# An encoder layer whose routing step is spread over the output projection, with another choice of the four experts and another first gather

## The chip, the core and the metric

One NeuronCore of a Trainium2 chip runs the whole layer in one launch. The metric is the time of that launch on the device in microseconds (us). The kernel before was timed three times: 1300.25, 1304.65 and 1307.12 us, so its median is 1304.65 us. TensorE is called PE here, VectorE DVE, ScalarE ACT, GpSimd POOL, and SP is the engine whose queue issues the weight loads.

## The reference

For 256 tokens x of 1024 features, the reference computes in fp32:

```
x = x + token_mixer(rmsnorm(x, g_mix), ...)      # SSD branch and attention branch, gated, then @ w_out
h = rmsnorm(x, g_ffn)
logits = h @ w_router + b_router                 # 256 x 32
top_val, top_idx = top_k(logits, 4)
top_w = softmax(top_val)
y[token] = sum over its 4 experts e of top_w * (act(h @ w_mlp1[e] + b_mlp1[e]) @ w_mlp2[e] + b_mlp2[e])
act(gate, up) = min(gate, 7) * sigmoid(1.702 * min(gate, 7)) * (clip(up, -7, 7) + 1)
out = rmsnorm(x + y, g_final)
```

The weights of the 32 experts are 32 x (1024x2048 + 1024x1024) fp32 numbers, 403 MB in all. Each is read once.

## The kernel before

**Two stages share one ring of weights.** `ring` holds 16 slots of 1 MB. The mixer works in 36 units (lines 433 and 436), each one slot of weights with 32 TensorE instructions; units 32 to 35 (`U_O` and up) are the output projection, and after each of them DVE adds half of the product to the residual rows `xres` (line 1162). The MoE stage works in 384 units, 12 for each expert: 8 "up" units (a slice of 128 rows of `w_mlp1`) and 4 "down" units (256 rows of `w_mlp2`). All of them are loaded by SP with `dma_start` at line 328. The first 16 loads wait for slots that the mixer gives up, the last of them for the end of unit 35. Load u+16 waits in `unit_used` (line 265) until TensorE has done its products with unit u. The loads stand in one queue in the order of the units.

**An expert on TensorE (lines 666 to 687).** It multiplies the 8 up units (line 629), transposes the result (line 663) once ACT has copied it out of PSUM (lines 906 and 908), adds the weighted result of the expert before to the sums in PSUM (`combine`, line 624), gathers the tokens of the next expert (line 611), and multiplies the 4 down units. The gather is a product of a 0/1 matrix `slotP` with three bf16 pieces (`hb1`, `hb2`, `hb3`) of the normed rows, 48 instructions.

**The routing step between the stages.** Everything in it waits for unit 35, in this order:

1. ACT squares the residual rows (line 883), POOL makes the reciprocal root (lines 953 and 954), DVE scales the rows into `hN` (line 1166).
2. PE transposes `hN` (line 416), DVE scales it with `g_ffn` into `hT` (line 995), PE multiplies the router (line 591).
3. DVE adds the bias, takes the eight largest of each row (line 1178), marks those above the fourth and those equal to it, and breaks ties with a scan (lines 1183 to 1196), which gives the mask `msk`.
4. PE counts the tokens of each expert with fp32 products (lines 596 to 600) and transposes the weights `wtok` (line 603). DVE subtracts for `hb3` (line 1206), turns the counts into ranks (lines 1209 to 1214) and places the tokens of expert 0 (lines 1227 to 1229).
5. ACT makes the three bf16 pieces in turn with DVE (lines 886, 888, 895, 1171, 1206).
6. PE gathers expert 0 (line 611), and then multiplies the weights with `b_mlp2` (line 698) into the four sums in PSUM. Only then begins the first up unit.

TensorE takes its instructions in order, so each item holds all that stand behind it. In the output projection it waits for all four parts of `hT` (`mix_ready`, 4) ahead of unit 32. DVE writes these parts in turn at lines 1153, 1154 and 1156. The last of ACT's transfers is `g_final` into `gfin` (line 899), issued after the third bf16 piece and the copy of the weights.

## Time and profile before

| what | us |
| --- | --- |
| median of the three timed runs | 1304.65 |
| span of the profiled execution | 1303.6 |
| the profiled execution's own time | not listed; the span is 1.05 below the median |
| PE busy | 1182.3 |
| DVE busy | 364.2 |
| ACT busy | 193.1 |
| POOL busy | 19.9 |

The span runs from the first to the last instruction. An engine's busy share is a mean over both stages. TensorE's instructions overlap each other, so a busy time of a line is not the time that the line takes; the difference of two start times is. An fp32 product is two instructions in the trace.

### The profile page before, as it was taken

What the parts mean: (1) busy time and instruction counts of PE and PEld (TensorE: products, weight loads), DVE (VectorE), ACT (ScalarE), POOL (GpSimd) and SP (SyncE); (2) the same over time, 40 slices, a digit from 0 to 9 for tenths busy, and PEclk for the clock granted to TensorE, in tenths of its full rate; (3) what the DMA queues carried; (4) which work ended last, traced back from release to release, by engine and by line L of the source; (5) the groups of instructions that cost most, each with busy time, mean ns of one, the idle gap of its engine ahead of it and who ended that gap; (6) DMA issues with size and microseconds to landing.
All of it is one profiled execution on the core that took longest, in us unless ns stands there. A gap on an engine that the chain in (4) does not pass through costs nothing.

```text
span 1303.6 us, 18034 instructions
## 1 busy us (share of the span) xinstructions
PE 1182.3 (91%) x6734; PEld 578.6 (44%) x6734; DVE 364.2 (28%) x1018; ACT 193.1 (15%) x362; POOL 19.9 (2%) x32
## 2 busy tenths in 40 slices
PE   5999999998799999989998988888899989998885
PEld 5888888887433333333333333333333333333331
DVE  2515788121412221222121111111122212111112
ACT  1212344001111110111011100100111011001001
POOL 0001111000000000000000000000000000000000
PEclk9999999999699999999999999999999999999998
DMA  9944322654099999999999999999999999999994
GB/s 283 281 142 117 128 97 97 230 217 171 29 417 417 417 417 417 417 417 418 417 418 418 418 418 418 418 418 417 417 417 418 418 418 418 418 418 417 418 417 178
DMA packets 113351, 445.18 MB, mean 342 GB/s; under 512 B 9731, under 2 KB 46947, under 8 KB 80515
## 3 DMA queue, kind: packets, MB, share of 16 engines
q1 hardware_dynamic: 109408, 441.48, 85.0%
q10 hardware_dynamic: 3907, 3.21, 0.9%
q8 instruction: 24, 0.39, 0.1%
q14 instruction: 12, 0.10, 0.0%
HBM read 443.61 MB, written 1.05 MB: 341 GB/s over the span
## 4 chain that ended last, share of the span: by engine, by line
PE 40%; DMA 37%; SPq 16%; issue 2%; DVE 2%; ACT 1%; ACTq 1%; DVEq 0%; POOL 0%; POOLq 0%
DMA ring<-in_w_mlp_dram 37%; SPq L328 16%; PE bank L433 14%; PE bank L629 14%; PE bank L436 5%; PE bank L624 1%; PE bank L611 1%; PE bank L562 1%; PE bank L552 1%; PE bank L698 1%; PE bank L524 1%; PE bank L416 1%; PE bank L663 0%; PE bank L591 0%; PE bank L515 0%
## 5 line engine op out<-in xcount | busy, mean ns | idle before, releaser
L629 PE MATMUL bank<-ring,arena 128*64 128x512 f32 x3072 | 702.7, 600 | 63.7 <-DMA ring<-in_w_mlp_dram 63.6
L629 PEld LDWEIGHTS bank<-ring,arena 128*64 128x64 f32 x3072 | 203.0, 137 | 515.3 <-issue 324.2
L1245 DVE TENSOR_TENSOR arena<-bank,b1T 128x256 f32<-128x256 f32 x128 | 53.8, 420 | 624.3 <-PE bank L663 621.9
L433 PE MATMUL bank<-hT,ring 128*128 128x256 f32 x576 | 128.3, 384 | 0.8 <-DVE hT L995 0.8
L433 PEld LDWEIGHTS bank<-hT,ring 128*128 128x128 f32 x576 | 110.9, 193 | 16.6 <-DVE hT L995 1.2
L436 PE MATMUL bank<-ring,hT 128*128 128x256 f32 x320 | 72.1, 386 | 2.2 <-DVE hT L1156 2.2
L906 ACT ACTIVATE arena<-bank 128x512 f32<-128x512 f32 x32 | 19.1, 597 | 362.4 <-PE bank L629 362.3
L436 PEld LDWEIGHTS bank<-ring,hT 128*128 128x128 f32 x320 | 61.5, 194 | 11.1 <-DVE hT L1156 2.6
L624 PE MATMUL bank<-arena 64*128 64x512 f32 x264 | 65.6, 615 | 0.8 <-ACT arena L916 0.8
L611 PEld LDWEIGHTS bank<-slotP,hb 128*128 128x128 bf16 x1536 | 47.7, 99 | 27.1 <-issue 23.5
L611 PE MATMUL bank<-slotP,hb 128*128 128x64 bf16 x1536 | 51.5, 195 | 3.1 <-DVE arena L1229 3.1
L663 PE MATMUL bank<-cst,arena 128*128 128x128 f32 x256 | 40.6, 286 | 14.4 <-ACT arena L906 9.6
L663 PEld LDWEIGHTS bank<-cst,arena 128*128 128x128 f32 x256 | 26.8, 140 | 47.1 <-ACT arena L906 36.1
L1227 DVE TENSOR_SCALAR slotP<-cst,rankm 128x64 bf16<-128x64 f32 x64 | 15.8, 247 | 96.9 <-ACT arena L914 96.9
L911 ACT ACTIVATE arena<-arena 128x256 f32<-128x256 f32 x64 | 26.7, 417 | 80.5 <-DVE arena L1248 80.4
L916 ACT ACTIVATE arena<-bank 128x512 f32<-128x512 f32 x32 | 19.1, 598 | 105.5 <-PE bank L629 105.5
L914 ACT ACTIVATE arena<-bank 128x256 f32<-128x256 f32 x32 | 12.3, 384 | 140.8 <-PE bank L618 140.8
L624 PEld LDWEIGHTS bank<-arena 64*128 64x128 f32 x264 | 22.7, 186 | 22.6 <-issue 20.9
L906 ACT ACT_TABLE_LOAD x8 | 10.3, 1283 | 134.4 <-PE bank L629 134.4
L433 PE MATMUL bank<-arena,ring 128*128 128x256 f32 x128 | 28.3, 380 | 0.5 <-ACT arena L867 0.5
L1251 DVE SCALAR_TENSOR_TENSOR arena<-arena 128x256 f32<-128x256 f32 x64 | 27.2, 426 | 2.4 <-DVE arena L1249 0.2
L433 PE MATMUL bank<-over,ring 128*128 128x256 f32 x128 | 27.8, 379 | 0.0
(204 smaller groups left out, 634.3 us busy)
## 6 DMA issues: line engine op xcount, KB each, us to landing
ring<-in_w_mlp_dram SPq DMA_DIRECT2D x384, 1024.0 KB, 22.1
ring<-in_w_in_dram SPq DMA_DIRECT2D x24, 1024.0 KB, 10.3
ring<-in_w_br_attn_dram SPq DMA_DIRECT2D x4, 1024.0 KB, 4.9
ring<-in_w_br_ssm_dram SPq DMA_DIRECT2D x4, 1024.0 KB, 5.0
ring<-in_w_out_dram SPq DMA_DIRECT2D x4, 1024.0 KB, 5.0
xres<-in_x_dram ACTq DMA_DIRECT2D x1, 1024.0 KB, 4.9
out_dram<-hN SPq DMA_DIRECT2D x2, 512.0 KB, 2.7
cst<-shape_constants_dram ACTq DMA_DIRECT2D x1, 736.0 KB, 6.4
```

Source lines behind the costliest of these rows:

```text
L328: sp.dma_start(dst, src).then_inc(slot_full[s], 16)
L433: last = nc.tensor.matmul(o, w[:, k, a * P:(a + 1) * P], rhs[:, k, :], start=(k == 0), stop=(k == KD - 1))
L436: last = nc.tensor.matmul(o, tokens[:, k, a * P:(a + 1) * P], w[:, k, :], start=(k == 0), stop=(k == KD - 1))
L611: last = nc.tensor.matmul(bank[b][:, k * CAP:(k + 1) * CAP], hb[part][:, t, k * P:(k + 1) * P], slotP[:, par, t, :], start=(t == 0 and par ...
L624: return nc.tensor.matmul(bank[b0 + q][:, :], slotWT[rows, (q // 2) * P:(q // 2 + 1) * P], ysb[rows, :], start=start, stop=stop, skip_grou ...
L629: return nc.tensor.matmul(bank[b][side * CAP:(side + 1) * CAP, :], tokens, w, start=start, stop=stop, skip_group_check=True)
L663: last = nc.tensor.transpose(bank[b][:, j * P:(j + 1) * P], hs[:, b * 512 + j * P:b * 512 + (j + 1) * P], ident)
L906: nc.scalar.activation(hs[:, 0:512], bank[0][:, :], ACT.Copy).then_inc(hs_ready, 1)
L911: nc.scalar.activation(sg[:, h * 256:(h + 1) * 256], ga[:, h * 256:(h + 1) * 256], ACT.Sigmoid, scale=ALPHA).then_inc(sg_ready, 1)
L916: nc.scalar.activation(ysb, bank[2][:, :], ACT.Copy).then_inc(ys_ready, 1)
L1245: step(V.tensor_tensor(o.rearrange("p (m s) -> p m s", m=4), bank[b][:, half].rearrange("p (m s) -> p m s", m=4), bias[:, m0:m0 + 4].unsqu ...
L1251: step(V.scalar_tensor_tensor(u_, u_, 1.0, g_, ALU.add, ALU.mult))
```

## The change

- Unit 32 takes its eight slices of `hT` as they come, two at a time (`first_out_unit`).
- The residual rows are transposed raw, in four quarters, and each quarter is multiplied with the router. The quarters stand in TensorE's order behind the units of the output projection, up to two units later. ACT squares each quarter as it comes, DVE copies and scales seven of the eight slices, ACT the last one.
- The norm's factor is applied to the logits, in the instruction that adds the bias, and not to the rows.
- The mask comes from two `match_replace` instructions and a comparison instead of comparisons, a sum, a scan and a product.
- The counts are bf16 products. Ranks are counted from 1, so the memset and the subtraction go.
- Expert 0 is gathered in one fp32 product from `xres` with a matrix `slot0` that carries the norm's factor, in two halves; the three bf16 pieces are wanted only from expert 1 on.
- The products with `b_mlp2` stand inside expert 0, in the place of its `combine` (which had added zeros), and TensorE waits there for the third bf16 piece. The transfer of `gfin` waits for that piece too.
- The first four experts are written out ahead of TensorE's loop.

```diff
...
+        lgt = lg36[:, :, 0:NE]
+        left36 = arena[:, 6984:7056].rearrange("p (t e) -> p t e", t=TT)
...
+        slot0 = slotW[:, 1, :, 0:CAP]
...
+        msk = sb("msk", [P, TT, NE], BF16, at=place_of["arena"] + 4 * 9488)
...
-            pe.wait_ge(mix_ready, 4)
-            for n in range(U_O, N_MIX):
-                unit(n, tokens=hT)
...
+            def first_out_unit():
...
+                for u in range(4):
+                    pe.wait_ge(mix_ready, u + 1)
+                    for a in range(2):
+                        for k in (2 * u, 2 * u + 1):
+                            last = nc.tensor.matmul(bank[n % 2][:, a * 256:(a + 1) * 256], hT[:, k, a * P:(a + 1) * P], w[:, k, :],
+                                                    start=(k == 0 and a == 0), stop=(k == KD - 1), skip_group_check=True)
+                last.then_inc(unit_done, 1)
+
+            def x1_transposes(u):
+
+                pe.wait_ge(unit_taken, U_O + u + 1)
+                for kk in range(2):
+                    o = bank[0][:, 0:256] if (u, kk) == (3, 1) else bank[2 + u][:, kk * 256:(kk + 1) * 256]
+                    for t in range(TT):
+                        last = nc.tensor.transpose(o[:, t * P:(t + 1) * P],
+                                                   xres[:, t, u * UW + kk * P:u * UW + (kk + 1) * P], ident)
+                last.then_inc(h2T_psum, 1)
...
+            def router(u):
+
+                pe.wait_ge(h2T_ready, u + 1)
+                for k in (2 * u, 2 * u + 1):
+                    if k == KD - 1:
+                        pe.wait_ge(x1T_last, 1)
+                    for t in range(TT):
+                        last = nc.tensor.matmul(bank[6][:, t * NE:(t + 1) * NE], x1T[:, k, t * P:(t + 1) * P], wr[:, k, :],
+                                                start=(k == 0 and t == 0), stop=(k == KD - 1), skip_group_check=True)
+                return last
+
+            first_out_unit()
+            unit(U_O + 1, tokens=hT)
+            x1_transposes(0)
+            unit(U_O + 2, tokens=hT)
+            x1_transposes(1)
             pe.wait_ge(late_in, 16 * 2)
-            for t in range(TT):
+            router(0)
+            unit(U_O + 3, tokens=hT)
+            x1_transposes(2)
+            router(1)
+            x1_transposes(3)
+            router(2)
+            router(3).then_inc(lg_psum, 1)
+
+            pe.wait_ge(msk_ready, 1)
+            nc.tensor.matmul(bank[7][:, 0:NE], m_leb[:, :], msk[:, 0, :], start=True, stop=True)
+            nc.tensor.matmul(bank[7][:, NE:2 * NE], onesb[:, :], msk[:, 0, :], start=True, stop=False)
+            nc.tensor.matmul(bank[7][:, NE:2 * NE], m_leb[:, :], msk[:, 1, :], start=False, stop=True).then_inc(rank_psum, 1)
+            nc.tensor.matmul(bank[4][:, 0:NE], onesb[:, :], msk[:, 0, :], start=True, stop=False)
+            nc.tensor.matmul(bank[4][:, 0:NE], onesb[:, :], msk[:, 1, :], start=False, stop=True).then_inc(cnt_psum, 1)
+
+            def first_gather():
+
+                pe.wait_ge(p_ready, 1)
                 for k in range(KD):
-                    last = nc.tensor.matmul(bank[6][:, t * NE:(t + 1) * NE], hT[:, k, t * P:(t + 1) * P], wr[:, k, :],
-                                            start=(k == 0), stop=(k == KD - 1))
-            last.then_inc(lg_psum, 1)
-
-            pe.wait_ge(w_ready, 1)
-            nc.tensor.matmul(bank[7][:, 0:NE], m_le, msk[:, 0, :], start=True, stop=True)
-            nc.tensor.matmul(bank[7][:, NE:2 * NE], ones, msk[:, 0, :], start=True, stop=False)
-            nc.tensor.matmul(bank[7][:, NE:2 * NE], m_le, msk[:, 1, :], start=False, stop=True)
-            nc.tensor.matmul(bank[7][:, 2 * NE:3 * NE], ones, msk[:, 0, :], start=True, stop=False)
-            nc.tensor.matmul(bank[7][:, 2 * NE:3 * NE], ones, msk[:, 1, :], start=False, stop=True)
...
-            for t in range(TT):
-                last = nc.tensor.transpose(bank[0][0:NE, t * P:(t + 1) * P], wtok[:, t, 0:NE], ident)
-            last.then_inc(wT_psum, 1)
+                    for t in range(TT):
+                        last = nc.tensor.matmul(bank[3 - k // 4][:, (k % 4) * CAP:(k % 4 + 1) * CAP], xres[:, t, k * P:(k + 1) * P],
+                                                slot0[:, t, :], start=(t == 0), stop=(t == TT - 1))
+                    if k == 3:
+                        last.then_inc(x0_psum, 1)
+                last.then_inc(x_psum, 1)
 
             def gather(par, b):
...
+
+                pe.wait_ge(wT_ready, 1)
+                pe.wait_ge(route_ready, 1)
+                for t in range(TT):
+                    for hf in range(2):
+                        nc.tensor.matmul(bank[SUMS + 2 * t + hf][:, :], wT[:, t * P:(t + 1) * P],
+                                         b2s[:, hf * 512:(hf + 1) * 512], start=True, stop=False, skip_group_check=True)
+
...
+                if first:
+                    pe.wait_ge(x0_half, 1)
+                else:
+                    pe.wait_ge(x32_ready, e + 1)
                 for q in range(KD):
+                    if first and q == 4:
+                        pe.wait_ge(x32_ready, e + 1)
                     up_unit(i, c, q)
                 for b in range(2):
                     pe.wait_ge(hs_ready, 2 * e + (b + 1))
                     transposes(b).then_inc(t_psum, 1)
-                pe.wait_ge(ys_ready, e + 1)
-                for q in range(4):
-                    combine(q)
...
+            for c in range(BODY):
+                expert(0, c, first=(c == 0))
...
+                act.wait_ge(unit_taken, U_O + u + 1)
+                for t in range(TT):
+                    nc.scalar.activation(hs[:, (2 * u + t) * UW:(2 * u + t + 1) * UW], xres[:, t, u * UW:(u + 1) * UW], ACT.Square,
+                                         accum_out=ssq[:, t, u:u + 1]).then_inc(x1sq_ready, 1)
+            act.wait_ge(h2T_psum, 4)
+            nc.scalar.activation(x1T[:, KD - 1, :], bank[0][:, 0:256], ACT.Copy,
+                                 scale=prmT[:, R_GFFN + KD - 1:R_GFFN + KD]).then_inc(x1T_last, 1)
+
+            act.wait_ge(x1r_ready, 1)
             for t in range(TT):
-                nc.scalar.activation(hN[:, t, :], xres[:, t, :], ACT.Square, accum_out=stat[:, 20 + t:21 + t]).then_inc(x1sq_ready, 1)
-
-            act.wait_ge(h2_ready, 2)
...
+            act.wait_ge(lmax_ready, 1)
+            for t in range(TT):
+                last = nc.scalar.activation(expl[:, t, :], lgt[:, t, :], ACT.Exp, bias=stat[:, 26 + t:27 + t])
+            last.then_inc(lexp_ready, 1)
+            act.wait_ge(wT_psum, 1)
+            nc.scalar.activation(wT[:, :], bank[6][0:NE, 0:SEQ], ACT.Copy).then_inc(wT_ready, 1)
             act.wait_ge(res_ready, 1)
             nc.scalar.activation(hb2[:, :, :], hs, ACT.Copy).then_inc(hb_ready, 1)
...
             nc.gpsimd.tensor_tensor(stat[:, 34:36], stat[:, 34:36], stat[:, 40:42], ALU.pow).then_inc(yr_ready, 1)
-            pool.wait_ge(x1sq_ready, 2)
+            pool.wait_ge(x1sum_ready, 1)
...
+            def x1T_copy(u):
+                dve.wait_ge(h2T_psum, u + 1)
+                kk = 2 if u < 3 else 1
+                V.tensor_tensor(x1T[:, 2 * u:2 * u + kk, :], bank[2 + u][:, 0:kk * 256].rearrange("p (k l) -> p k l", k=kk),
+                                prmT[:, R_GFFN + 2 * u:R_GFFN + 2 * u + kk].unsqueeze(2).to_broadcast([P, kk, SEQ]),
+                                ALU.mult).then_inc(h2T_ready, 1)
+
+            V.memset(slotWT, 0.0).then_inc(pw_ready, 1)
+            V.memset(lg36[:, :, NE:NE + 4], NO_LOGIT)
+            V.tensor_copy(m_leb[:, :], m_le)
+            V.tensor_copy(onesb[:, :], ones)
...
+                if u >= 1:
+                    x1T_copy(u - 1)
+            dve.wait_ge(x1sq_ready, 2 * 4)
+            V.tensor_reduce(stat[:, 20:22], ssq[:, :, :], AXX, ALU.add).then_inc(x1sum_ready, 1)
+            x1T_copy(3)
...
+            dve.wait_ge(lg_psum, 1)
+            dve.wait_ge(vec_in, 16 * 7)
             for t in range(TT):
...
+                last = V.scalar_tensor_tensor(lgt[:, t, :], bank[6][:, t * NE:(t + 1) * NE], r_tok[t], brt_b, ALU.mult, ALU.add)
+            link(last)
             for t in range(TT):
                 last = V.max(top8[:, t, :], lgt[:, t, :])
...
+            V.tensor_scalar(stat[:, 26:28], top8[:, :, 0:1].rearrange("p t a -> p (t a)"), -1.0, None, ALU.mult).then_inc(lmax_ready, 1)
+            link(V.memset(top8[:, :, TOPK:8], NO_LOGIT))
...
+                last = V.match_replace(left36[:, t, :], top8[:, t, :], lg36[:, t, :], PICKED)
+            link(last)
+            V.tensor_tensor(msk[:, :, :], left36[:, :, 0:NE], lgt, ALU.not_equal).then_inc(msk_ready, 1)
+
+            dve.wait_ge(msk_ready, 1)
+            dve.wait_ge(rank_psum, 1)
+            link(V.tensor_tensor(rankm[:, :, 0:NE], bank[7][:, 0:2 * NE].rearrange("p (t e) -> p t e", t=TT), msk[:, :, :], ALU.mult))
...
+                last = V.tensor_scalar(slot0[:, t, :], iota, rankm[:, t, 0:1], r_tok[t], ALU.is_equal, ALU.mult)
+            last.then_inc(p_ready, 1)
+
...
-            dve.wait_ge(hb_ready, 2)
-            V.tensor_tensor(hs3, hs3, hb2[:, :, :], ALU.subtract).then_inc(res_ready, 1)
...
+            def first_tokens(h, psum_sem):
+                dve.wait_ge(psum_sem, 1)
+                return V.tensor_tensor(x32[:, 4 * h:4 * h + 4, :], bank[3 - h][:, 0:256].rearrange("p (k s) -> p k s", k=4),
+                                       prmT[:, R_GFFN + 4 * h:R_GFFN + 4 * h + 4].unsqueeze(2).to_broadcast([P, 4, CAP]), ALU.mult)
+
+            def first_residual(t):
+                dve.wait_ge(hb_ready, 1)
+                return V.scalar_tensor_tensor(hs3[:, t, :], xres[:, t, :], r_tok[t], hb1[:, t, :], ALU.mult, ALU.subtract)
+
+            first_tokens(0, x0_psum).then_inc(x0_half, 1)
+            first_residual(0)
+            first_tokens(1, x_psum).then_inc(x32_ready, 1)
+            first_residual(1).then_inc(res_ready, 1)
...
+            dve.wait_ge(cnt_psum, 1)
...
```

## Rows read from the trace of the kernel before

**Rows 1.** The page: GB/s in 40 slices of the span, 32.6 us each.

```profile
GB/s 283 281 142 117 128 97 97 230 217 171 29 417 417 417 417 417 417 417 418 417 418 418 418 418 418 418 418 417 417 417 418 418 418 418 418 418 417 418 417 178
```

**Rows 2.** Busy times by stretch: stretch, us; PE, PEld, DVE, ACT, POOL; granted clock, DMA share, GB/s.

```profile
358.00:416.00 58.00, 56.60 (x348) 21.33 (x346) 12.51 (x38) 8.47 (x14) 0.00 (x0) 1.00 1.02 416
...
1196.00:1256.00 60.00, 54.66 (x330) 19.11 (x328) 12.28 (x37) 6.02 (x12) 0.00 (x0) 1.00 1.02 417
```

**Rows 3.** The issues of weight loads around the routing step, in order of time.

```profile
319.35 0.33 SPq L328 DMA_DIRECT2D ring<-in_w_mlp_dram  x1
...
355.87 21.75 SPq L328 DMA_DIRECT2D ring<-in_w_mlp_dram  x10
```

**Rows 4.** The chain of waits, in order of time: start, us, what.

```profile
1248.52 26.19 DMA ring<-in_w_mlp_dram
```

**Rows 5.** TensorE from the output projection to expert 0: start, us, line, count [idle].

```profile
289.73 29.58 PE L436 MATMUL bank<-ring,hT 128*128 128x256 f32 x128 [2.23 <-DVE hT L1156]
...
324.83 3.42 PE L416 MATMUL bank<-cst,hN 128*128 128x128 f32 x16 [5.51 <-DVE hN L1166]
...
336.89 0.63 PE L596 MATMUL bank<-arena,cst 128*128 128x32 f32 x2 [2.83 <-DVE arena L1196]
...
339.04 0.61 PE L603 MATMUL bank<-cst,wtok 128*32 128x128 f32 x2
342.74 2.74 PE L611 MATMUL bank<-slotP,hb 128*128 128x64 bf16 x48 [3.08 <-DVE arena L1229]
345.41 7.19 PE L698 MATMUL bank<-arena 32*128 32x512 f32 x8
352.53 15.24 PE L629 MATMUL bank<-ring,arena 128*64 128x512 f32 x64
368.97 1.15 PE L663 MATMUL bank<-cst,arena 128*128 128x128 f32 x8 [1.21 <-ACT arena L906]
370.05 1.99 PE L624 MATMUL bank<-arena 64*128 64x512 f32 x8
...
373.47 3.65 PE L629 MATMUL bank<-ring,arena 128*64 128x512 f32 x16
```

**Rows 6.** The router's products alone at either clock (PE, PEld, clock, DMA).

```profile
329.00:331.20 2.20, 2.17 (x20) 2.17 (x20) 1.00 0.00 0
331.30:334.10 2.80, 2.76 (x14) 2.63 (x13) 0.50 0.00 0
```

**Rows 7.** The columns of rows 2, in stretches of one us around changes of the clock.

```profile
290.00:291.00 1.00, 1.00 (x4) 0.85 (x4) 0.00 (x0) 0.00 (x0) 0.00 (x0) 0.65 0.97 401
...
293.00:294.00 1.00, 1.00 (x4) 0.79 (x4) 0.00 (x0) 0.00 (x0) 0.00 (x0) 0.64 1.05 430
...
355.00:356.00 1.00, 1.00 (x6) 0.29 (x4) 0.00 (x0) 0.00 (x0) 0.00 (x0) 0.92 0.00 0
```

**Rows 8.** DVE, POOL and ACT in the routing step, in order of time.

```profile
319.35 0.69 DVE L1162 SCALAR_TENSOR_TENSOR xres<-bank,xres 128x512 f32<-128x512 f32 x1 [6.21 <-PE bank L436]
...
322.63 0.70 POOL L954 TENSOR_TENSOR stat<-stat 128x2 f32<-128x2 f32 x1
...
334.36 0.29 DVE L1178 MAX8 arena<-arena 128x8 f32<-128x32 f32 x2
...
336.16 0.41 DVE L1194 SCALAR_TENSOR_TENSOR arena<-arena,stat 128x32 f32<-128x32 f32 x2
336.61 0.22 DVE L1196 TENSOR_TENSOR arena<-arena 128x64 f32<-128x64 f32 x1
...
337.85 2.29 DVE L1206 TENSOR_TENSOR arena<-arena,hb 128x2048 f32<-128x2048 f32 x1
340.18 1.91 ACT L895 ACTIVATE hb<-arena 128x2048 bf16<-128x2048 f32 x1 [4.18 <-DVE arena L1206]
...
341.55 0.30 DVE L1228 TENSOR_SCALAR arena<-cst,rankm,wtok 128x64 f32<-128x64 f32 x1
```

**Rows 9.** Groups of instructions by shape: ACT's, 256 wide, with a sum.

```profile
L847 ACT ACTIVATE arena<-bank,stat 128x256 f32<-128x256 f32 x16 | 7.4, 470 | 24.7 <-DVE stat L1104 24.7
```

More of the change, by code:

```diff
@@ L38 @@
 NEG = -1e30
+NO_LOGIT = -3e38
+PICKED = -2e38
 UW = 256
@@ L674, in expert @@
                     transposes(b).then_inc(t_psum, 1)
-                pe.wait_ge(ys_ready, e + 1)
-                for q in range(4):
-                    combine(q)
+                if first:
+                    bias_products()
+                    pe.wait_ge(hb_ready, 3)
+                else:
+                    pe.wait_ge(ys_ready, e)
+                    for q in range(4):
+                        combine(q)
                 if not final:
@@ L687, in expert @@
                     down_unit(i, c, q)
-            pe.wait_ge(p_ready, 1)
-            pe.wait_ge(hb_ready, 3)
-            gather(0, 3).then_inc(x_psum, 1)
-            pe.wait_ge(wT_ready, 1)
+            first_gather()
+            pe.wait_ge(w_ready, 1)
             for t in range(TT):
-                for hf in range(2):
-                    if t == 1 and hf == 1:
-                        pe.wait_ge(route_ready, 1)
-                    nc.tensor.matmul(bank[SUMS + 2 * t + hf][:, :], wT[:, t * P:(t + 1) * P],
-                                     b2s[:, hf * 512:(hf + 1) * 512],
-                                     start=True, stop=False, skip_group_check=True).then_inc(b2_psum, 1)
-            with pe.Fori(0, NE // BODY - 1) as i:
+                last = nc.tensor.transpose(bank[6][0:NE, t * P:(t + 1) * P], wtok[:, t, 0:NE], ident)
+            last.then_inc(wT_psum, 1)
+            for c in range(BODY):
+                expert(0, c, first=(c == 0))
+            with pe.Fori(1, NE // BODY - 1) as i:
                 for c in range(BODY):
-                    expert(i, c, False)
+                    expert(i, c)
             for c in range(BODY):
-                expert(NE // BODY - 1, c, c == BODY - 1)
-            pe.wait_ge(ys_ready, 1 + NE)
+                expert(NE // BODY - 1, c, final=(c == BODY - 1))
+            pe.wait_ge(ys_ready, NE)
             pe.wait_ge(pw_ready, NE + 1)
@@ L1224, in place @@
                     if shift:
[L1225 to L1226 removed]
+                        link2(V.tensor_scalar(shifted[:, t:t + 1], rk, -float(shift), None, ALU.add))
+                        rk = shifted[:, t:t + 1]
                     V.tensor_scalar(slotP[:, c % 2, t, :], iota, rk, None, ALU.is_equal)
@@ L1264, in gate_up @@
                 step(V.scalar_tensor_tensor(ub, ub, 1.0, ga, ALU.add, ALU.mult))
-            place(0, 0).then_inc(p_ready, 1)
-            dve.wait_ge(x_psum, 1)
-            tokens_in(3).then_inc(x32_ready, 1)
-            dve.wait_ge(b2_psum, 4)
-            V.memset(ysb, 0.0).then_inc(ys_ready, 1)
             def expert(i, c, final):
```

97 lines of the change are left out of this document (39 added, 58 removed).

## Prediction, made before the changed kernel ran

> **What bounds the kernel now.** I read the traffic first. From slice 12 to the last but one the core reads 417 or 418 GB/s, and in slice 11 only 29 [rows 1]. The busy times by stretch say the same more closely: 416 GB/s from 358 us, 417 near the end, the DMA engines busy throughout (share 1.00 to 1.02) [rows 2]. So the MoE stage is one stream of weight loads, also in the first 150 us of it, where TensorE is the engine that looks busy. The issues of the loads give its ends: the sixteenth load of the MoE stage goes out at 319.35 us, when the mixer is done, and the seventeenth at 355.87, when the first up unit has been used [rows 3]. In the chain of waits the last load lands at 1248.52 + 26.19 = 1274.7 [rows 4]. 368 loads in 1274.7 - 355.9 = 918.8 us are 2.50 us each. After that stand 1303.6 - 1274.7 = 28.9 us of last expert, sums and norm, which the change leaves alone.
>
> TensorE does not hold this stream back once it runs: eight up units took 15.24 us and two down units 3.65 [rows 5], 1.8 to 1.9 us a unit against 2.50. So the span is (first reissue) + 918.8 + 28.9, plus any stall of the stream, and the reader has to follow one time: the end of the first up unit. Between 319.35 and 352.53 TensorE goes through the routing step; each wait in it is in TensorE's timeline [rows 5] and its makers in that of the other engines [rows 8].
>
> **Part 1, ahead of the end of the projection.** TensorE waits 2.23 us for the fourth part of hT [rows 5]. With the parts taken in turn the first three cover 24 of 32 instructions, 5.2 us, and the fourth is there 2.2 us after the start, so the wait is gone: -2.23. The granted clock falls from 2.4 to 1.2 GHz within 290 to 291 and is back within 293 to 294 [rows 7], behind that wait, so unit 32 is slow: the four units took 29.58 us, and at the 6.91 us between the ends of the later ones they would take 27.6. Without the idle time I expect no fall: -1.96. Moved in front of the end: two quarters of transposes (4 instructions at 0.144 from 8 in 1.15 [rows 5], 0.58 each) and one quarter of the router (8 instructions at 0.12 from about 18.5 in 2.20 at full clock [rows 6], 0.98): +2.14. DVE's and ACT's new work here (a copy of 0.69, two squares) fits into units of 6.9 us. The new memset and casts on DVE stand where it waits for unit 32. The projection ends at 319.35 - 4.19 + 2.14 = 317.3.
>
> **Part 2, to the logits.** Two more quarters of transposes and three of router, 2 x 0.58 + 3 x 0.98 = 4.10. Beside it: DVE adds unit 35 in 0.69 [rows 8]; ACT squares it in two instructions of 0.47 and two reads of about 0.2, so at 2.1 after the end [rows 9]; a reduction; POOL 0.19 and 0.70 with gaps [rows 8], at 3.3. The last copies, 256 wide, take 0.4 on DVE and ACT after the transposes at 2.2, so 2.7. All are ahead of 4.1. Half of this could run at 1.2 GHz, where the router's instruction took 2.80 / 14 = 0.20 [rows 6]; the worst would be +2.2. TensorE is at it without a gap, so I add 0.3: logits at 321.7. The norm of the rows (DVE, 1.42) and the wait for it go from the path.
>
> **Part 3, the choice.** DVE: two products with bias 0.41 and two maxima 0.29 [rows 8], negation and memset 0.17 and 0.11 (the smallest instructions of this listing), two match_replace, comparison 0.22 [rows 8], and six gaps of 0.03. The trace has no match_replace. A scan of eight largest over as many elements is 0.15; two of them are the lower end (0.29 for both), twice that the upper (0.58). I take 0.42, between them. Sum 1.80: mask at 323.5. The same stretch took 2.75 before.
>
> The Trainium skill (VectorE: DVE Perf Modes, Two Vector instructions with no wait between them) counts a match_replace as two instructions, a load of the values and the replacement; its Vector Engine (DVE) Microarchitecture Reference gives about 75 ns for each instruction and 1.04 ns a column. An estimate by these pages is 4 x 0.075 + 88 x 0.00104 = 0.39 us; no run here shows it yet, and the sum goes by the rows.
>
> TensorE counts with three bf16 products instead of fp32 ones: between 0.3 and the 1.3 of three fp32 ones (0.43 from start to start of two lines with 5 between 336.89 and 339.04 [rows 5]); with the way into and out of PSUM I take 0.55. DVE: ranks 0.23, two placements of 0.30 that overlap, 0.5 [rows 8]. Expert 0 can be gathered at 324.9.
>
> **Part 4, the first gather.** 16 fp32 products, 32 instructions instead of 48 bf16 ones. The nearest rows are the router's (same stationary tile of 128x128, 32 columns, 0.12 and 0.20 us an instruction at the two clocks [rows 6]) and the transposes' (3.42 / 16 = 0.21 at 1.2 GHz [rows 5], 128 columns). So 6.4 to 6.8 us at 1.2 GHz and 3.9 to 4.6 at 2.4; the bf16 gather took 2.74 [rows 5]. TensorE has stood idle for most of 3 us, and before it ran the same stretch at 1.2 GHz: I take 6.5, all at that clock. This step costs more than it did, and it stands bare. The weights' transposes, 0.61 [rows 5], follow. DVE's copy of either half (0.4) fits under them and under the gather; the residual between the two copies, half of a 2.29 instruction [rows 8], fits too. First up unit: 332.0, against 352.53.
>
> The Trainium skill (FP8 and Floating Point Precision, TensorE Precision Notes) has an fp32 product as four passes through the array. By passes alone 64 of them with 64 columns at 1.2 GHz would be an estimate of 3.4 us. The router's rows disagree: there four passes of 32 columns would be 0.11 us a product, and the product took 0.40. If the pages' count held the result would be 3 us earlier.
>
> **Part 5, where the 7.19 us of bias products go.** At the start they were bare [rows 5]. Inside expert 0 they run at 2.4 GHz, half of 7.19, 3.6, in the place of 1.99 of combine [rows 5]: the gap between the last up unit and the first down unit grows by 1.6. Before, unit 8 was used at 373.47 + 1.8 = 375.3, when the stream had eight loads, 20.0 us, from 355.9 on, so work until 375.9: a cover of 0.6. Now the stream would stand 1.0. But the gfin transfer of 0.5 MB, which was in the idle time, now joins the stream: 0.5 / 417 GB/s = 1.3 us, and it lies in the same hole. Together +1.4. Its wait for the third bf16 piece: copy of DVE residual 1.1, ACT 1.91, DVE 2.29, ACT 1.91 and small instructions [rows 8] end about 15 us after the gather began, at 340; TensorE comes to that wait at 351. Behind the waiting ACT stand only copies for expert 0 that are wanted at 347, so 7 us of cover; without it each us late is a us on TensorE there.
>
> **The sum.** The first up unit at 1.2 GHz takes 355.87 - 352.53 = 3.3 us with the issue, so the reissue comes at 335.3. The clock rose 2.6 us after the start of the up units before; it may come later now, and I add 0.6. Span: 335.3 + 0.6 + 918.8 + 1.4 + 28.9 = 1285.0, that is 18.6 less than 1303.6. The span is 1.05 below the median, so I forecast 1286.0.
>
> **Rivals.**
>
> A. The clock is back before or inside the gather. For it: up units brought it back within 2.6 us, and the gather uses the whole array as they do. Against it: 2.8 us of router products with the same stationary tile, at 0.50 throughout, did not [rows 6], nor did 7.19 us of bias products; it rose in 355 to 356 [rows 7]. Gather 1 to 2 us shorter, first unit 1.6 shorter, smaller hole: 3 to 4 us more gain, about 1282.
>
> B. Expert 0 gives back a part: TensorE begins it at 1.2 GHz and stays there for most of the eight up units, 3.4 us each against 2.5 for a load. Each such unit beyond the first stands the stream 0.9, and the hole before unit 8 grows by what is lost: with six units about 8 us, 1294. For it: the clock rose in 355 only after 12 us of unbroken work. Against: most of that was bias products, and up units raised it in under 3 us.
>
> C. The other side. The clock stays at 1.2 GHz through experts, because the stream then starves TensorE and the idle time keeps the clock down. At 0.9 us a unit the gain of 18.6 is used up after 20 units, near the end of expert 1; 30 units, half of expert 2 included, cost 27 us and end 8 above before, at 1313. Against it: waits for loads in the late stage (TensorE busy 54.66 of 60) go with a clock of 1.00 [rows 2].
>
> D. The stream isn't moved: the 16 loads in the ring or the memory limit it elsewhere, and the 18 us become idle time later. The rate of 417 GB/s after the ramp in every slice [rows 1] speaks against it. About 1302.
>
> **How the numbers follow.** Chances: forecast (1281 to 1290.5) 0.66, A 0.12, B 0.12, C 0.03, D 0.07. Ends of the unknown costs: match_replace and counts -0.4 to +1.0, router's clock -0.3 to +1.9, gather -0.3 to +0.4, and the runs before spread by 7 us, so a median by perhaps 2. The range 1280 to 1294 takes in A and most of B. Faster or slower means by over 0.5%, 6.5 us, about what can be told from no change: faster 0.91 (forecast, A, nearly all of B), within 0.06, slower 0.03.
>
> **What would show it.** Right: no idle time and no fall of the clock at unit 32; a first reissue near 336; then 417 GB/s in each slice to the end; 29 us after the last landing. Each step has its line: logits 4.4 us after the last addition's unit, mask 1.8 later, gather of 6 to 7 us, a gap of 7.3 between unit 7 and unit 8 with a short dip of the traffic. Wrong: a reissue at 336 with a span over 1290 (B or D), or TensorE waiting on the third piece in expert 0.

## The result

The changed kernel took 1286.86 us at the median of four runs (1283.51 to 1289.42); the kernel before took 1305.75 beside it (1300.25 to 1307.12). The ratio is 0.986, with an interval of 0.9835 to 0.9886. The forecast was 1286.0.

The span of the profiled execution is 1284.2 us against 1303.6. On its page the stream runs at the rate of [rows 1] from slice 12 on, and slice 11, which had 29 GB/s, has 214:

```profile
GB/s 282 289 134 128 132 98 99 200 203 224 214 416 417 416 418 416 418 417 417 419 417 418 418 417 417 417 417 417 418 418 419 418 418 419 417 419 417 418 416 176
```

The first reissue of a weight load, which answers to the second of [rows 3] at 355.87 (start, us, what):

```profile
334.06 23.46 SPq L339 DMA_DIRECT2D ring<-in_w_mlp_dram  x10
```

The last landing, which answers to [rows 4]: 1229.99 + 25.36 = 1255.35.

```profile
1229.99 25.36 DMA ring<-in_w_mlp_dram
```

TensorE from the projection to expert 0, for [rows 5]. L603 is the new unit 32, L613 the quarters of transposes, L624 the router, L643 the counts, L654 the first gather, L683 the products with expert weights, L726 the bias products:

```profile
286.89 7.07 PE L603 MATMUL bank<-ring,hT 128*128 128x256 f32 x32
...
316.29 0.60 PE L613 MATMUL bank<-cst,xres 128*128 128x128 f32 x4
316.73 0.98 PE L624 MATMUL bank<-wr,hN 128*128 128x32 f32 x8
317.54 0.64 PE L613 MATMUL bank<-cst,xres 128*128 128x128 f32 x4
318.01 1.87 PE L624 MATMUL bank<-wr,hN 128*128 128x32 f32 x16
321.72 0.21 PE L643 MATMUL bank<-msk,m_leb 128*128 128x32 bf16 x1 [1.83 <-DVE msk L1271]
...
322.94 7.09 PE L654 MATMUL bank<-arena,xres 128*128 128x64 f32 x32 [0.91 <-DVE arena L1277]
329.81 0.63 PE L764 MATMUL bank<-cst,wtok 128*32 128x128 f32 x2
330.38 15.58 PE L683 MATMUL bank<-ring,arena 128*64 128x512 f32 x64
...
348.24 3.69 PE L726 MATMUL bank<-arena 32*128 32x512 f32 x8
351.87 1.57 PE L665 MATMUL bank<-slotP,hb 128*128 128x64 bf16 x48
353.37 3.65 PE L683 MATMUL bank<-ring,arena 128*64 128x512 f32 x16
```

Three pieces make up a span, and each can be read in any profile of this kernel: the time x0 at which the last unit of the gated branches ends (DVE's fourth start at line 1153 before), the way from there to the first reissue, and the stream from the reissue to the last landing. What follows, 28.9 us, was the same in all fourteen profiles to 0.1 (the two kernels' and twelve of the runs below).

| kernel | x0 | x0 to reissue | stream | span |
| --- | --- | --- | --- | --- |
| before | 287.54 | 68.33 | 918.84 | 1303.6 |
| changed | 287.09 | 46.97 | 921.29 | 1284.2 |
| difference | -0.45 | -21.36 | +2.45 | -19.4 |

x0 lies ahead of the first instruction that the change moves. It was 285.1 to 285.5 in five profiles and 287.1 to 288.0 in nine, so the 2 us between these belong to no edit, and single spans are compared below by the other two columns.

The way of 47.0 against 68.3, by start to start on TensorE: x0 to the end of unit 35, 29.2 against 31.8; from there to the gather, 6.65 against 23.4; the gather 6.9 against 2.7; what stands between it and the first up unit 0.6 against 7.1; the first up unit with the issue 3.7 against 3.3.

The 23.4 us from unit 35 to the gather were 14.7 to the end of the router, 2.8 to the mask and 5.9 to the gather; now they are 3.6, 1.8 and 1.3. So most of the gain, 11.1 us, lies where the norm of the rows and the whole transposes and router stood.

### The profile page after: what moved, and what is told of

Its sections match the earlier page's. It is cut to its first block, busy times and chain, and to the rows that moved or that the text cites. A ratio compares the mean times of both kernels' runs of the same rounds, so it can differ in the third digit from the quotient of the medians.

```text
span 1284.2 us, 17971 instructions
## 1 busy us (share of the span) xinstructions
PE 1174.3 (91%) x6705; PEld 575.0 (45%) x6705; DVE 361.7 (28%) x1014; ACT 195.3 (15%) x376; POOL 19.9 (2%) x32
## 3 DMA queue, kind: packets, MB, share of 16 engines
HBM read 443.61 MB, written 1.05 MB: 346 GB/s over the span
## 4 chain that ended last, share of the span: by engine, by line
PE 42%; DMA 34%; SPq 18%; issue 2%; ACT 1%; DVE 1%; ACTq 1%; DVEq 0%; POOL 0%; POOLq 0%
DMA ring<-in_w_mlp_dram 34%; SPq L339 17%; PE bank L683 16%; PE bank L444 14%; PE bank L447 4%; PE bank L678 1%; PE bank L665 1%; PE bank L573 1%; PE bank L563 1%; PE bank L654 1%; PE bank L535 1%; PE bank L603 1%; PE bank L717 0%; SPq L275 0%; PE bank L427 0%
## 5 line engine op out<-in xcount | busy, mean ns | idle before, releaser
L683 PE MATMUL bank<-ring,arena 128*64 128x512 f32 x3072 | 703.5, 600 | 63.9 <-DMA ring<-in_w_mlp_dram 63.8
L683 PEld LDWEIGHTS bank<-ring,arena 128*64 128x64 f32 x3072 | 203.0, 137 | 515.3 <-issue 322.5
L447 PE MATMUL bank<-ring,hT 128*128 128x256 f32 x288 | 63.8, 380 | 0.0
L447 PEld LDWEIGHTS bank<-ring,hT 128*128 128x128 f32 x288 | 54.2, 190 | 7.1
L665 PEld LDWEIGHTS bank<-slotP,hb 128*128 128x128 bf16 x1488 | 45.1, 98 | 23.5 <-issue 23.5
L665 PE MATMUL bank<-slotP,hb 128*128 128x64 bf16 x1488 | 48.8, 193 | 0.0
L717 PEld LDWEIGHTS bank<-cst,arena 128*128 128x128 f32 x256 | 26.8, 140 | 47.1 <-ACT arena L980 36.1
L980 ACT ACT_TABLE_LOAD x8 | 10.3, 1283 | 117.4 <-PE bank L683 117.4
L1348 DVE TENSOR_TENSOR arena<-arena 128x256 f32<-128x256 f32 x64 | 27.2, 425 | 2.3
```

The lines of the kernel that those rows point to most:

```text
L447: last = nc.tensor.matmul(o, tokens[:, k, a * P:(a + 1) * P], w[:, k, :], start=(k == 0), stop=(k == KD - 1))
L665: last = nc.tensor.matmul(bank[b][:, k * CAP:(k + 1) * CAP], hb[part][:, t, k * P:(k + 1) * P], slotP[:, par, t, :], start=(t == 0 and par ...
L683: return nc.tensor.matmul(bank[b][side * CAP:(side + 1) * CAP, :], tokens, w, start=start, stop=stop, skip_group_check=True)
L717: last = nc.tensor.transpose(bank[b][:, j * P:(j + 1) * P], hs[:, b * 512 + j * P:b * 512 + (j + 1) * P], ident)
L980: nc.scalar.activation(hs[:, 0:512], bank[0][:, :], ACT.Copy).then_inc(hs_ready, 1)
L1348: V.tensor_tensor(u_, u_, s_, ALU.mult).then_inc(actT_ready, 1)
```

## The experiments

The kernel before was timed anew beside each group of runs; its medians were 1303.79, 1303.04 and 1304.19 us there and 1305.75 above. So medians of different groups are compared to no better than about 2 us, and "the changed kernel" below is the 1286.86 of the result.

**Unit 32 takes hT in parts.** The kernel before, with this alone:

```diff
-            pe.wait_ge(mix_ready, 4)
-            for n in range(U_O, N_MIX):
...
+            first_out_unit()
+            for n in range(U_O + 1, N_MIX):
                 unit(n, tokens=hT)
```

> The kernel before, with one edit: unit 32 takes the four parts of hT as they come. My theory: TensorE's wait of 2.23 us goes, and with it the fall of the clock that cost 1.96, so the projection ends at 315.2 instead of 319.35, the first reissue of a weight load comes at 351.7 instead of 355.87, the stream stays 918.8 us long, and the span is 1299.4, 4.2 less. Rival: the clock falls anyway somewhere in the projection; then 2.2 less, 1301.4. Rival D (the stream is not moved by an earlier routing step): span 1303 to 1304 with a reissue at 351.7.

Measured: 1297.69 against 1303.79, ratio 0.9954 (0.9938 to 0.997). To the reissue 61.1 us, 7.3 less; stream 918.6. The wait and the fall of the clock behind it are gone, 4.2 us as worked out. The other 3 come from further on, in TensorE's timeline of this run:

```profile
341.21 3.92 PE L712 MATMUL bank<-arena 32*128 32x512 f32 x8
345.06 15.65 PE L643 MATMUL bank<-ring,arena 128*64 128x512 f32 x64
```

The bias products took 3.92 where they took 7.19 in [rows 5]: the mean clock of 341 to 345 was 0.91, and it was back at 0.50 from 346 to 348. So the clock changes at other points of the same instructions here. Whether these 3 us belong to the edit is open: all five runs of this kernel had a mean clock of 0.987 and are 6.1 us below the kernel before at the median, where its fourteen runs had 0.983 to 0.986, so something beyond the 4.2 seems to go with the edit, and no run says by what path. The stream moved with its start: rival D is out.

**Bias products inside expert 0.** The kernel before, with the products in the place of the first combine:

```diff
+                if first:
...
+                    pe.wait_ge(route_ready, 1)
...
+                else:
+                    pe.wait_ge(ys_ready, e)
+                    for q in range(4):
+                        combine(q)
```

> The kernel before, with one edit: the products with b_mlp2 stand inside expert 0 in the place of its combine, as in the change; the transfer of gfin stays in the idle time. My theory: the first up unit 7.1 us earlier, at 345.4 (TensorE waits 0.7 for the tokens, so 346.2); the reissue at 349.6; the gap between unit 7 and unit 8 grows from 5.7 to 7.4 us, so the stream stands about 1.0 us in it. Span 1303.6 - 6.3 + 1.0 = 1298.3. Rival: the bias products had been what brought the clock back; then the up units stay at 1.2 GHz longer, the reissue still comes at 349.6, but units 1 to 3 take 3.4 us each and the span is 1301 or more.

Measured: 1303.59 against 1303.79, ratio 0.9997 (0.9985 to 1.0008): no difference that can be told, a miss. The way to the reissue was 5.7 us shorter, but the stream 923.2, 4.3 longer; the 1.4 us that this leaves lie within the interval. In the gap between the last up and the first down unit (busy times by stretch, the columns of [rows 2]; then TensorE):

```profile
366.00:370.00 4.00, 4.00 (x54) 2.92 (x54) 1.96 (x5) 0.25 (x1) 0.00 (x0) 0.57 0.96 375
```

```profile
366.52 2.74 PE L611 MATMUL bank<-slotP,hb 128*128 128x64 bf16 x48
369.19 3.94 PE L629 MATMUL bank<-ring,arena 128*64 128x512 f32 x16
```

The clock fell in the gap, the gather took 2.74 instead of 1.57, and the first down unit was used 23.5 us after the first reissue; before it was 19.4.

**The first gather from bf16 pieces again.** The changed kernel, with expert 0's `first_gather` replaced by `gather(0, 3)` behind the third piece, and `slot0` by `slotP`. The weights' transposes stand ahead of it, in the wait, and the tokens are made as before:

```diff
-            first_gather()
...
+            pe.wait_ge(p_ready, 1)
+            pe.wait_ge(hb_ready, 3)
+            gather(0, 3).then_inc(x_psum, 1)
```

> The changed kernel, with expert 0 gathered again from the three bf16 pieces, so its gather waits for the third one. My theory: the third piece comes at about 332.3, the gather takes 2.7 at 1.2 GHz, the tokens 0.7, so the first up unit starts at 335.8 instead of 330.4 and the span is 5.4 longer than that of the changed kernel, 1289.6. Rival: the fp32 gather, which took 7.09 us instead of 2.74, gives back most of what it saves in waiting: 1 to 2 us, 1286.

Measured: 1293.56, ratio to before 0.9918 (0.989 to 0.9945). 5.6 us more to the reissue, as expected, and a stream of 923.4: the clock fell in expert 0's gap here too, and the gather in it took 2.74. TensorE waits 8.08 us for the piece and gathers in 2.72:

```profile
332.59 2.72 PE L665 MATMUL bank<-slotP,hb 128*128 128x64 bf16 x48 [8.08 <-ACT hb L967]
```

**The whole router behind the projection.** The changed kernel, in this order, with DVE's first three copies behind its last addition:

```diff
             unit(U_O + 1, tokens=hT)
-            x1_transposes(0)
             unit(U_O + 2, tokens=hT)
-            x1_transposes(1)
-            pe.wait_ge(late_in, 16 * 2)
-            router(0)
             unit(U_O + 3, tokens=hT)
+            x1_transposes(0)
+            x1_transposes(1)
+            router(0)
             x1_transposes(2)
```

> The changed kernel, with all four quarters of transposes and router products behind the last unit of the projection. My theory: TensorE does the same instructions in the same total time, only the waits for DVE's copies are new; the logits are 0.5 us later, span 1284.7. That the quarters stand among the units would be worth only that. Rival: spreading is the source of the gain of the routing step; then the logits are 2.1 us later (the part that stood ahead of the last unit's end comes bare) and the clock, which falls sooner, adds 1 more: 1287.3.

Measured: 1286.7 (1286.66 to 1288.49), ratio 0.9878 (0.9857 to 0.9898). The logits come 0.8 us later after x0, with one wait of 0.60 for DVE's first copy, and the reissue 0.5. So spreading the quarters over the units buys 0.5 us, and is not where most of the gain lies. The norm of the rows ahead of the transposes, which is gone in both orders, was the 5.51 of idle time in [rows 5]; no run puts it back alone.

**Bias products ahead of expert 0 in the changed kernel.**

```diff
+            bias_products()
             for c in range(BODY):
                 expert(0, c, first=(c == 0))
```

> The changed kernel, with the products with b_mlp2 moved back ahead of the first up unit. My theory: they stand bare; at 1.2 GHz 7.2 us, a part of it under nothing, so the reissue comes at 341.3 instead of 334.06, less about 1 us that expert 0's gap gave to the stream; 1293. Rival (from the kernel before with only this edit, which moved nothing: 1303.59 against 1303.79): what is won ahead of expert 0 is lost inside it, where the clock falls in the longer gap; then 1287 to 1289, and the gap of expert 0 is under 4 us at 2.4 GHz.

Measured: 1292.62, ratio 0.9915 (0.9892 to 0.9939). 9.1 us more to the reissue, the stream 2.0 shorter, and 5.8 us over the changed kernel at the median, 7.1 by these two columns. Beside the 7.16 of products stands a wait for the counts' last cast, which I had left out:

```profile
332.79 7.16 PE L726 MATMUL bank<-arena 32*128 32x512 f32 x8 [1.85 <-DVE over_i L1304]
```

So the move of these products, worth 0.2 us at the median and 1.4 by the columns in the kernel before, is worth 5.8 and 7.1 beside the others. Why is under "What sets the stream".

**gfin issued in the mixer.**

```diff
             act.dma_start(b2s, b_mlp2[0]).then_inc(late_in, 16)
+            act.wait_ge(y_psum, 8)
+            act.dma_start(gfin, g_final.partition_broadcast(P)).then_inc(gfin_in, 16)
```

> The changed kernel, with the gfin transfer issued in the mixer, where the DMA engines stand idle, instead of inside the stream. My theory: the stream (first reissue to last landing) was 921.3 us against 918.8 before, and gfin is 1.3 to 2 of the difference; without it the stream stands for 0.9 us ahead of unit 8 instead, so the gain is about 1 us, 1285.9. Rival: the transfer lay wholly in the hole ahead of unit 8 and cost nothing: 1286.9, with a hole in the traffic of 1.3 us or more.

Measured: 1289.33, ratio 0.9888 (0.9864 to 0.9912), 2.5 us over the changed kernel: a miss. The way to the reissue is the same, 47.1; the stream is 924.5. The clock fell in expert 0's gap, so the ninth load went out 24.8 us after the reissue instead of 21.4, and the traffic is under 80 GB/s for 3 us. So this run doesn't price the transfer. TensorE, then two stretches of one us:

```profile
353.49 2.74 PE L665 MATMUL bank<-slotP,hb 128*128 128x64 bf16 x48
```

```profile
358.00:359.00 1.00, 1.00 (x6) 0.32 (x4) 0.00 (x0) 0.00 (x0) 0.00 (x0) 0.60 0.03 12
359.00:360.00 1.00, 1.00 (x6) 0.28 (x4) 0.00 (x0) 0.00 (x0) 0.00 (x0) 1.00 0.00 0
```

**Three filler products.** Two behind the router and one behind the counts:

```diff
+            def filler(n):
+                for _ in range(n):
+                    nc.tensor.matmul(bank[1][:, 0:256], ident, cst[:, 0:256], start=True, stop=True)
+
+            filler(2)
```

> The changed kernel with three products added that nothing reads (128x128 by 256 columns of a constant, into bank 1): two behind the router, one behind the counts, where TensorE stood idle 1.83 and 0.91 us. Theory: the idle time keeps the clock at 1.2 GHz; with work there it rises before or early in the gather, which then takes about 4.5 us instead of 7.09, and the first up unit starts at 2.4 GHz: the reissue 3 to 4 us sooner, 1283. Rival: the fillers are too little to raise it, and delay the counts: reissue 0 to 0.5 later, 1287.

Measured: 1287.11 (1286.92 to 1287.54), ratio 0.9877 (0.9854 to 0.9899), no gain. The clock held to 325 and fell early in the gather, which took 5.9; the reissue came 1.9 us sooner, and the fall in the gap took it back (stream 923.4). That the fillers held the clock to 325 isn't shown: in the run with the router behind, without fillers, it held to 324.2.

**Bias products between up units 5 and 6.**

```diff
                     up_unit(i, c, q)
+                    if first and q == 5:
+                        bias_products()
```

> The changed kernel with the products with b_mlp2 between up units 5 and 6 of expert 0 instead of in its gap. Theory: the gap between the last up and the first down unit shrinks from 7.3 to 3.7 us, so the clock no longer falls in it in any run and the stream never stands; the up units, 1.72 us against 2.5 of a load, have room for 3.7 us. About 1 us less on the median, 1285.5 to 1286, and a smaller spread over the runs (before 1283.5 to 1289.4). Rival: the gap is not what the runs differ by; the same median and spread.

Measured: 1286.03 (1285.31 to 1287.44), ratio 0.9872 (0.9848 to 0.9895). The clock did not fall in the gap and the spread is 2.1 us instead of 5.9, as expected. The stream is no shorter, 922.3: the room that I saw between 1.72 and 2.5 us a unit is the cover for the gap, and the products spend it wherever they stand.

**The same in the kernel before.** The four products of the second experiment moved between up units 5 and 6.

> The kernel before, with the products with b_mlp2 between up units 5 and 6 of expert 0; gfin stays in the idle time, everything else as before. When they stood in the gap instead, the same removal of 7.2 us ahead of expert 0 moved nothing (1303.59 against 1303.79). Theory: that was because the clock fell in the gap (366 to 369 us) and the stream stood there; here the gap is 3.7 us, so the stream starts about 6 us earlier and keeps it: 1297.5 to 1298.5. Rival: the bias products ahead of expert 0 were worth nothing for another reason (they only filled a wait, or helped the clock up): 1302 to 1304 again.

Measured: 1302.5 against 1304.19, ratio 0.9984 (0.997 to 0.9999). My theory fails: 62.5 to the reissue, 5.8 less, and a stream of 923.1 at 2.4 GHz throughout the gap. So the fall of the clock alone does not explain the longer stream. TensorE's work from the first reissue to the end of the first down unit is 23.1 us here and 23.5 with the products in the gap, against 19.4 before, and the ninth load waits for it.

**Both edits in the changed kernel**, bias products between the units and gfin in the mixer.

> The changed kernel with two edits: bias products between up units 5 and 6, and the gfin transfer issued in the mixer. With the first alone 1286.03; the second alone showed a hole of 3 us in the traffic and 1289.33. Theory: without the fall of the clock in the gap there is no hole, so the 1.3 to 2 us of the transfer come off the stream: first reissue to last landing 919 to 920 instead of 922.3, 1284.3. Rival: the transfer doesn't lengthen the stream; 1286 and 922.

Measured: 1285.36 (1284.42 to 1285.82), ratio 0.9857 (0.9835 to 0.9879). To the reissue 47.1, stream 922.6, as long as with gfin's transfer in it (922.3). That doesn't mean that the transfer costs nothing: see the next section.

**Fillers until the mask, and the weights' transposes behind the first up unit**, on top of both.

```diff
+            filler(4)
...
+                    if first and q == 0:
+                        pe.wait_ge(w_ready, 1)
+                        ...
```

> The two edits of the run before, and two more: four filler products behind the router and one behind the counts (with two and one the clock held until 325 us and fell early in the gather), and the transposes of the weights behind the first up unit instead of ahead of it. Theory: the clock stays at 2.4 GHz through the gather (4.3 us instead of 7.09) and the first up unit (1.7 instead of 3.3), and 0.57 of transposes leave the path: reissue near 328 instead of 332 to 334, 1280. Rival: the gather, with 64 columns a product, does not hold the clock: it falls within it as before and the gain is 0.6 to 1.5 us, 1283.

Measured: 1281.82 (1281.41 to 1283.97) against 1304.19, ratio 0.9837 (0.9814 to 0.9861), the lowest of all. 41.6 us to the reissue, 5.4 less than the changed kernel. TensorE's timeline:

```profile
317.96 1.97 PE L644 MATMUL bank<-cst 128*128 128x256 f32 x8
...
321.17 3.79 PE L660 MATMUL bank<-arena,xres 128*128 128x64 f32 x32 [0.39 <-DVE arena L1286]
324.88 1.94 PE L689 MATMUL bank<-ring,arena 128*64 128x512 f32 x8
```

Line 644 is the fillers. The clock was 1.00 from 312 to 339, the gather took 3.7 instead of 6.9, the first up unit with the issue 2.1 instead of 3.7. Of these 5.4 us the stream gives 2.7 back (924.0): the clock fell after all, at 339.5, behind the bias products, and the last two up units took 5.35 us instead of 3.65. All four runs have a mean clock of 0.995 or 0.996 where the run before has 0.991 in all four, so the fillers' effect is not one profile's chance; the 0.57 of transposes is in the 5.4 too.

**The old choice in the changed kernel**, the comparisons, sum, scan and product of before, one profile.

> The changed kernel with the choice of the four experts made as before (comparisons, sum, scan, product) instead of by match_replace. Theory: from the logits to the mask 2.7 us instead of 1.67, all of it bare, so the counts and the first reissue come 1.0 later. Rival: ACT's exponentials or its bf16 pieces are what ends last there; then the gather starts as early as in the changed kernel.

Measured: 2.92 us from the logits to the mask against 1.67, the first up unit 1.25 later. The reissue is 0.7 later, since the clock rose in the first up unit here. The gather starts 1.24 later too, so ACT does not end last.

## What sets the stream

Load u+16 waits for unit u, so eight loads go out while TensorE does the eight up units, and the ninth waits for the first down unit. The time that the eight loads last is the cover of the prediction. The trace has each packet of the weight loads. "Behind" is by how much later than in the kernel before, counted from the first reissue, the same number of bytes of weights has landed, at 14 and at 40 us after the reissue:

| kernel | gfin among the loads | ninth load out | behind at 14 | behind at 40 | stream |
| --- | --- | --- | --- | --- | --- |
| before | no | 19.7 | 0 | 0 | 918.8 |
| hT in parts | no | 19.7 | 0.2 | 0.2 | 918.6 |
| changed, bias ahead | no | 19.2 | 0.1 | 0.1 | 919.3 |
| bias between, gfin early | no | 22.7 | 0.5 | 3.3 | 922.6 |
| before, bias between | no | 23.4 | 0.5 | 3.7 | 923.1 |
| bf16 pieces | no | 23.5 | 0.4 | 4.0 | 923.4 |
| before, bias inside | no | 23.8 | -0.1 | 3.9 | 923.2 |
| all | no | 24.5 | 0.5 | 4.7 | 924.0 |
| gfin early | no | 24.8 | 0.8 | 5.2 | 924.5 |
| changed | yes | 21.4 | 2.2 | 2.2 | 921.3 |
| router behind; old choice | yes | 21.4 | 2.0; 2.0 | 2.0; 1.9 | 920.9; 921.2 |
| bias between | yes | 22.4 | 2.2 | 2.7 | 922.3 |
| fillers | yes | 24.6 | 2.0 | 4.3 | 923.4 |

**gfin's transfer.** In the five kernels where its packets run among the weight loads, from 7.5 to 12.8 us after the reissue, the loads are 2.0 to 2.2 us behind at 14; in the nine others at most 0.8. Its 0.5 MB at 417 GB/s are 1.3 us. In the changed kernel, where it is issued at 337.92, the traffic itself is low for two us (the columns of [rows 2], here and below):

```profile
338.00:339.00 1.00, 1.00 (x8) 0.35 (x6) 0.00 (x0) 0.00 (x0) 0.00 (x0) 1.00 1.23 246
339.00:340.00 1.00, 1.00 (x8) 0.35 (x6) 0.00 (x0) 0.00 (x0) 0.00 (x0) 1.00 0.64 254
```

Why it costs more than its bytes isn't settled.

**The ninth load.** Without gfin among them, the stream loses nothing while it is out by 19.7 us, and from 22.7 on about what it is later than 20.0: 2.7 late, 2.8 lost; 3.5 and 3.6; 3.8 and 4.0; at the far end 4.8 and 4.4. With gfin the eight loads last some 2 us longer, and so does the cover: nothing lost at 21.4, 0.5 at 22.4, 2.3 at 24.6. In the changed kernel the ninth load goes out at 355.44, and there is no hole:

```profile
355.00:356.00 1.00, 1.00 (x7) 0.29 (x4) 0.00 (x0) 0.00 (x0) 0.00 (x0) 1.00 1.04 414
```

With gfin early and the products between the units it goes out at 355.26, and there is one:

```profile
355.00:356.00 1.00, 1.00 (x8) 0.40 (x6) 0.99 (x2) 0.00 (x0) 0.00 (x0) 1.00 0.16 66
356.00:357.00 1.00, 1.00 (x6) 0.20 (x2) 0.00 (x0) 0.00 (x0) 0.00 (x0) 1.00 1.03 135
```

So the transfer and a late ninth load hide each other: without the transfer the same TensorE work leaves a hole of nearly the same length, and the stream is as long (922.3 and 922.6). An estimate for gfin early with the clock at 2.4 GHz in the gap: 21.4 - 20.0 = 1.4 us lost instead of 2.2. No run has this. It also says why the move of the bias products was worth so little in the kernel before: there it put the ninth load from 19.7 to 23.8, beyond the cover; in the changed kernel from 19.2 to 21.4, within the cover that gfin gives, so only the transfer's 2 us came back.

Up to 0.8 us more falls later in the stream, and isn't placed. In two kernels with the products between the units, the seventh load is late as well (15.1 us after the reissue in the kernel before, where it was 10.3 without the move), and the traffic there falls to 180 to 360 GB/s for 4 us ahead of the hole. No run separates this.

## Why the prediction was right

The steps of the sum, each against the profile:

1. The bound. The span is the first reissue plus the stream plus 28.9 us. Right: in fourteen profiles the end took 28.9, and the streams differ by what they lost in their first 40 us, to within 0.8.
2. The projection: end of unit 35 29.8 us after x0 forecast, 29.2 measured. No idle time and no fall of the clock at unit 32. The new quarters cost 0.44 and 0.81 from start to start where I had 0.58 and 0.98, durations of groups that overlap their neighbours.
3. To the logits 4.4 forecast, 3.6 measured: the same overlap, and the 0.3 for the clock was not needed; it fell at 320, just behind the router. From the mask to the gather the terms (0.55, 0.23, 0.5) add up to 1.28, and it took 1.29; the 324.9 is 0.1 more than they give.
4. The mask 1.80 forecast, 1.67 measured. The unknown instruction, from DVE's timeline:

```profile
320.98 0.09 DVE L1269 MATCH_VALUE_LOAD arena<-arena 128x8 f32 x1
321.06 0.18 DVE L1269 MATCH_REPLACE8 arena<-arena 128x36 f32<-128x36 f32 x1
...
321.43 0.22 DVE L1271 TENSOR_TENSOR msk<-arena 128x64 bf16<-128x64 f32 x1
```

Both choices took 0.42 from 320.98 to 321.40, the value taken. They are two instructions each, as the Trainium skill (VectorE: DVE Perf Modes, Two Vector instructions with no wait between them) has it. The prediction's estimate of 0.39 from the other page is near.

5. The gather 6.5 forecast, 6.9 measured at 1.2 GHz, and 3.7 at 2.4 in the run with everything. The router's rows were the right price. The estimate by four passes (Trainium skill, FP8 and Floating Point Precision, TensorE Precision Notes), 3.4 at 1.2 GHz, does not hold here.
6. The third piece 15 us after the gather began: it ended at 337.89, 15.0 after, and TensorE came to its wait at 351.9.

```profile
335.98 1.91 ACT L970 ACTIVATE hb<-arena 128x2048 bf16<-128x2048 f32 x1 [2.36 <-DVE arena L1312]
```

7. Expert 0: the gap of 7.3 was 7.4, and the cover of 20.0 us for eight loads fits the runs. The price was wrong: I had 1.4 us for a hole ahead of unit 8 with gfin's 1.3 in it (the text doesn't say how 1.0 and 1.3 make 1.4), and the stream grew by 2.5. There was no hole. gfin's transfer alone put the loads 2.2 us behind, 14 us after the reissue, so the mis-sized term is the transfer.

To the reissue I had 48.4 us after x0 (with 0.6 for a late clock), and it was 47.0; the stream was 1.1 longer than forecast. The two misses, of steps 2 and 3 and of step 7, nearly cancel, so the 1286.0 is closer than its parts deserve. The last step, 1.05 us from the span to the median, set a span beside times of other executions: in every later run the span is 1.8 to 2.1 below the time of the same execution.

Of the rivals, B was half real: the up units did not stay slow, but the clock does fall in expert 0's gap in some runs, and there the stream stands. Such runs can explain the spread of 1283.5 to 1289.4. The runs speak for it without showing it: from the shortest to the longest the four runs have mean clocks of 0.992, 0.991, 0.989 and 0.988; with the products between the units all four have 0.991, and the spread is 2.1 us. A, a clock that is back for the gather, did not come by itself (0.50 from 321 to 333); it needed work for TensorE in the waits. C and D did not come.

## What to carry to other kernels

Where one stream of transfers bounds a stage, an earlier start is worth its full time only while the consumer's work on the first slots stays shorter than the transfers already queued; work pushed behind the start spends that cover. Count it before and after a move, since the same edit was worth 0.2 us alone and 5.8 beside the others. A small transfer that moves from idle time into the stream adds its time, and hides a late consumer by as much; so when the stream is longer, look when the loads fall behind, and not only how late the consumer was. And a step that waits less can still be slow for another reason, TensorE's clock: five short useless products ahead of the gather kept it at 2.4 GHz there, and three did not.

## What was not expected of the hardware

In the routing step the clock fell at 320 us with TensorE busy to 319.9 by transposes and products of 32 columns (the columns of [rows 2]):

```profile
320.00:321.00 1.00, 0.00 (x0) 0.00 (x0) 0.88 (x7) 1.00 (x2) 0.00 (x0) 0.52 0.55 229
333.00:334.00 1.00, 1.00 (x6) 0.37 (x4) 0.39 (x2) 0.62 (x1) 0.00 (x0) 0.66 0.00 0
```

It rose again at 333.7, 3.3 us into the up units, though the gather and the transposes had kept TensorE busy from 322.9 on. With four 256-column products behind the router and one behind the counts it stayed at 2.4 GHz through the same gather. The point of the fall moves between kernels with the same instructions there: with the router behind the projection, TensorE stood idle for the same 1.83 us ahead of the counts and the clock held to 324.2. The bias products, 32 rows deep, ran at 1.2 GHz for 7.19 us in one profile [rows 5] and mostly at 2.4 in another (3.92), with the same instructions ahead of them from unit 33 on.
